# Expert rows gated in the activation and added to the stream in DRAM by accumulating indirect stores

## The chip, the cores and the metric

The kernel runs on one core of a Trainium2 chip. The metric is the device time of one execution in microseconds, 1139.73 before (median of three).

The engines are named as in the profile: PE (TensorE; PEld is its weight load), DVE (VectorE), ACT (ScalarE), POOL (GpSimd) and SP (SyncE). Each runs its own instructions in order and waits for the others by semaphores. SP, ACT and POOL can issue DMAs; an indirect DMA, whose rows go to or come from addresses in a table, is issued by POOL here.

## What is computed

One layer of a decoder for 1024 prompt rows and 64 sample rows of width 1024: a token mixing, a cross-attention, a mixture of experts and a final norm. Only the last two are touched.

```python
def hierarchical_moe(h, ...):          # h = rmsnorm(x, g_ffn)
    g_idx, g_p = top-1 of softmax over 4 expert groups
    top_v, top_i = lax.top_k(logits of the group's 4 experts, 2)
    top_w = jax.nn.softmax(top_v, axis=-1) * g_p
    gates = (one_hot(expert_id, 16) * top_w[..., None]).sum(axis=1)
    hg, hu = t @ w_gate[e], t @ w_up[e]           # 1024 -> 256
    a = jax.nn.silu(hg) * hu * gates
    return (a @ w_down[e]).summed over e          # 256 -> 1024

x = x + hierarchical_moe(rmsnorm(x, g_ffn), ...)
y = rmsnorm(x, g_final)
```

## The kernel before

The rows are held as NT = 9 tiles of 128 (the last one with 64 real rows) in the SBUF tensor X, the residual stream. The program is five blocks, each closed by a barrier of all engines: mixing, attention, routing, experts, combine.

**Routing** normalises X into xs, stores it to h_rows in DRAM (SP) and computes the router's logits. Each row goes to two experts, so there are 2176 pairs. They are sorted by expert into tiles of 128 slots, each expert beginning a tile of its own; at least MIN_TILES = 17 and at most NTILE = 32 tiles can be in use (27 are, with these inputs), and the slots left over are padding. The result is a set of small tables: IDX (the row of h_rows that each slot takes, by a matmul of the one-hot matrices big and A, line 1475), POS (the slot in which each row's two results lie), WT (the two gates of each row) and TAB (per tile: whether it starts an expert, its weights' row, whether it is in use, when the buffer is free, and the number of stores).

**Experts** works in steps, one for each tile. For tile j, POOL gathers 128 rows of h_rows into one of the two buffers of xg (`fetch`, line 1696, which waits until the tile two before is transposed), PE transposes them (`turn`, line 1822), ACT and DVE split them into a high and a low part (lines 1725 and 1785), PE multiplies by the gate and up weights (`gate_up`), ACT and DVE form a = silu(hg)*hu (lines 1740 and 1802), PE transposes a (`turn_a`, line 1845), and multiplies by the down weights (`down`). ACT copies the result into one of two buffers of y (lines 1756 and 1758) and issues its store to y_rows (line 1763). On PE step s is turn(s+1), gate_up(s), down(s-1), turn_a(s). Where a tile starts an expert, 3 MB of weights are loaded by SP in three pieces (line 1688) and split by ACT (line 1719) and DVE (line 1780) into Wh and Wl, pieces by pieces between the other work of ACT and DVE. The steps are written out for the first four tiles, then stand in loops of two steps for the rest up to 29, and again written out; from step 16 on each is skipped if its tile is empty. Each loop body begins with reads from TAB and a branch.

**Combine** has for each of the nine tiles of X: two gathers from y_rows by POS (POOL, line 1929), two multiply-adds into X with the gates WT (DVE, line 1959), a square sum (ACT, line 1950), two small operations for the norm (POOL), one for the output o (DVE, line 1969) and a store (SP).

So that combine reads defined values of y_rows, mixing ends with two copies from an input into the part of y_rows that may be left unwritten (SP, line 208).

Of the kernel before, what the change touches and what calls it, by code (L numbers as in the profile page):

```python
# [86 lines left out]
def mixing_block(nc, io, keep, y_dram):  # L87
# [10 lines left out]
    with ExitStack() as ctx:  # L98
# [32 lines left out]
        fill_st = sem("fill_st")  # L131
# [33 lines left out]
        def _(sp):  # L165
# [44 lines left out]
            sp.wait_ge(fill_st, 16 * -(-(NTILE - MIN_TILES) // NT))  # L210
# [1120 lines left out]
def routing_block(nc, io, keep, h_dram):  # L1331

    with ExitStack() as ctx:
# [3 lines left out]
        POS, WT, IDX, TAB = (keep[n] for n in ("pos", "wt", "idx", "tab"))  # L1337
# [25 lines left out]
        A = sb("A", [P, K2, NTILE])  # L1363
# [4 lines left out]
        ones_ok, h_st = sem("ones_ok"), sem("h_st", XB)  # L1368
# [68 lines left out]
        def _(pe):  # L1437
# [36 lines left out]
            for i in range(K2):  # L1474
                last = pe.matmul(ps[:, 5, 0:NTILE], big[:, i, :], A[:, i, :], start=(i == 0), stop=(i == K2 - 1))
# [3 lines left out]
        def _(dve):  # L1479
# [52 lines left out]
            then(v(WT[:, 0, :], m["gp"][:, :], m["rden"][:, :], ALU.mult))  # L1532
            then(v(WT[:, 1, :], WT[:, 0, :], m["ex"][:, :], ALU.mult))
# [33 lines left out]
            for k in range(2):  # L1567
# [12 lines left out]
            then(dve.tensor_copy(POS[:, :], pf[:, :]))  # L1580
# [3 lines left out]
            then(v(A[:, :, :], bcast(tt[:, :], NTILE), itile.rearrange("p (o n) -> p o n", o=1).to_broadcast(  # L1584
                [P, K2, NTILE]), ALU.is_equal))
            for k in range(2):
                last = v(A[:, k * NT:(k + 1) * NT, :], A[:, k * NT:(k + 1) * NT, :], bcast(tok[:, 0, :], NTILE), ALU.mult)
# [21 lines left out]
            then(r(used[:, 0:2], tef[:, :].rearrange("p (t o) -> p o t", o=2), AX_X, ALU.add))  # L1609
            then(dve.tensor_scalar(TAB[:, 4, 0:2], used[:, 0:2], 16.0, None, ALU.mult))  # L1610
            dve.wait_ge(idx_ps, 1)
            dve.tensor_copy(IDX[:, :], ps[:, 5, 0:NTILE])
# [12 lines left out]
def experts_block(nc, io, keep, h_dram, y_dram):  # L1625
# [10 lines left out]
    with ExitStack() as ctx:  # L1636
        sem = Sems(nc, keep["all"], "e")
        sb = lambda n, s, d=F32: ctx.enter_context(nc.sbuf_tensor("e_" + n, s, d))
        ps, ident, IDX, TAB = (keep[n] for n in ("ps", "ident", "idx", "tab"))
# [7 lines left out]
        x_ld, y_st = sem("x_ld", 2), sem("y_st", 2)  # L1647
# [17 lines left out]
        def tile_steps(eng, emit):  # L1665
# [5 lines left out]
            for s in range(4):  # L1671
                emit(s, s)
            for lo, hi, each in ((4, MIN_TILES - 1, emit), (MIN_TILES - 1, NTILE - 2, unless_empty)):
                with eng.Fori(0, (hi - lo) // 2) as i:
                    for u in range(2):
                        each(2 * i + (lo + u), 4 + u)
            for s in range(NTILE - 2, NTILE + 1):
                unless_empty(s, s)
# [12 lines left out]
        def _(pool):  # L1691
# [6 lines left out]
            for j in range(NTILE):  # L1698
                if j < MIN_TILES + 2:
                    fetch(j)  # L1700
                else:
                    with pool.If(started(pool, j - 2) >= 1):
                        fetch(j)

        @block.scalar
        def _(act):
# [26 lines left out]
            def step(s, like):  # L1733
# [27 lines left out]
                if like >= 1:  # L1761
                    act.wait_ge(y_ok, 2 * (s - 1) + 2)
# [3 lines left out]
            for par in range(2):  # L1766
                act.wait_ge(y_st[par], stores[par])
# [318 lines left out]
```

## Time and profile before

| | us |
|---|---|
| median of three runs (1139.54 to 1144.16) | 1139.73 |
| the profiled execution | 1139.48 |
| its span, first to last instruction | 1137.7 |
| mixing and attention | 680 |
| routing | 69 |
| experts | 333 |
| combine | 56 |

The stages are read off the timeline, at the first instruction of each block. Over the span PE is busy 83%, DVE 43%, ACT 36% and POOL 12%, and PE's granted clock is 0.924 of full speed in the mean.

The rows further down come from several views: busy time in a stretch of time; a timeline of single instructions with the idle time before each and what ended it; and groups of instructions. "issue" as a releaser means that the engine waited for nothing the profile shows. DMA times run from issue to landing.

### The profile page before, as it was taken

What the parts mean: (1) busy time and instruction counts of PE and PEld (TensorE: products, weight loads), DVE (VectorE), ACT (ScalarE), POOL (GpSimd) and SP (SyncE); (2) the same over time, 40 slices, a digit from 0 to 9 for tenths busy, and PEclk for the clock granted to TensorE, in tenths of its full rate; (3) what the DMA queues carried; (4) which work ended last, traced back from release to release, by engine and by line L of the source; (5) the groups of instructions that cost most, each with busy time, mean ns of one, the idle gap of its engine ahead of it and who ended that gap; (6) DMA issues with size and microseconds to landing.
All of it is one profiled execution on the core that took longest, in us unless ns stands there. A gap on an engine that the chain in (4) does not pass through costs nothing. (4 is left out here: it accounts for less than half of the span.)

```text
span 1137.7 us, 14742 instructions
## 1 busy us (share of the span) xinstructions
PE 938.6 (83%) x4691; PEld 763.3 (67%) x4692; DVE 484.3 (43%) x646; ACT 406.1 (36%) x657; POOL 134.7 (12%) x181
## 2 busy tenths in 40 slices
PE   4899959999989878989999989269999988769600
PEld 3689848688847665878888867158787866548500
DVE  3441373412124464733322224655554545455156
ACT  5442202300036665522111115035565545444212
POOL 3210000000011100000000004021121211001064
PEclk9999979999999989999999999659999988989955
DMA  6311010591047856100000004256868676656177
GB/s 229 146 45 64 36 44 19 236 390 40 1 170 247 309 218 259 57 28 1 1 1 1 1 1 167 78 216 221 288 249 297 232 267 219 261 204 221 56 252 256
DMA packets 40565, 171.25 MB, mean 151 GB/s; under 512 B 4971, under 2 KB 5371, under 8 KB 31658
## 3 DMA queue, kind: packets, MB, share of 16 engines
q1 hardware_dynamic: 26754, 112.74, 27.2%
q0 software_dynamic: 9872, 43.68, 11.0%
q10 hardware_dynamic: 3888, 14.16, 3.1%
q8 instruction: 32, 0.52, 0.2%
q14 instruction: 19, 0.16, 0.1%
HBM read 144.57 MB, written 33.96 MB: 157 GB/s over the span
## 5 line engine op out<-in xcount | busy, mean ns | idle before, releaser
L1780 DVE TENSOR_TENSOR e_Wl<-raw,e_Wh 128x2048 f32 x48 | 109.9, 2292 | 116.6 <-ACT e_Wh L1719 116.6
L1719 ACT CAST e_Wh<-raw 128x2048 f32 x48 | 91.7, 1912 | 95.2 <-issue 51.3
L534 PE MATMUL ps<-a_wh,a_hTh 128*128 128x512 f32 x288 | 115.8, 402 | 3.8 <-DVE a_wl L372 2.4
L535 PE MATMUL ps<-a_wh,a_hTl 128*128 128x512 f32 x288 | 113.7, 395 | 0.0
L536 PE MATMUL ps<-a_wl,a_hTh 128*128 128x512 f32 x288 | 113.5, 394 | 0.0
L1619 PE MATMUL ps<-e_Wh,e_xTh 128*128 x224 | 93.5, 418 | 0.0
L1620 PE MATMUL ps<-e_Wl,e_xTh 128*128 x224 | 90.1, 402 | 0.0
L1621 PE MATMUL ps<-e_Wh,e_xTl 128*128 x224 | 89.6, 400 | 0.0
L1696 POOL DMA_INDIRECT e_xg<-h_rows,idx x29 | 48.6, 1677 | 295.7 <-PE ps L1822 247.3
L534 PEld LDWEIGHTS ps<-a_wh,a_hTh 128*128 128x128 f32 x288 | 55.2, 192 | 15.5 <-DVE a_wl L372 2.8
L536 PEld LDWEIGHTS ps<-a_wl,a_hTh 128*128 128x128 f32 x288 | 55.0, 191 | 11.8
L535 PEld LDWEIGHTS ps<-a_wh,a_hTl 128*128 128x128 f32 x288 | 55.2, 192 | 11.1
L1822 PE MATMUL ps<-ident,e_xg 128*128 128x128 f32 x232 | 36.8, 310 | 22.2 <-issue 13.9
L1100 PE MATMUL ps<-t_QKh,t_hTh 128*128 128x512 f32 x128 | 50.6, 396 | 3.0 <-DVE t_hTl L988 2.4
L1100 PE MATMUL ps<-t_VOh,t_pTh 128*128 128x512 f32 x128 | 50.5, 395 | 2.4 <-DVE t_pTl L988 2.4
L1621 PEld LDWEIGHTS ps<-e_Wh,e_xTl 128*128 128x128 f32 x224 | 43.9, 196 | 9.9
L1619 PEld LDWEIGHTS ps<-e_Wh,e_xTh 128*128 128x128 f32 x224 | 44.3, 198 | 8.4
L1102 PE MATMUL ps<-t_QKl,t_hTh 128*128 128x512 f32 x128 | 49.9, 390 | 0.0
L1102 PE MATMUL ps<-t_VOl,t_pTh 128*128 128x512 f32 x128 | 49.9, 390 | 0.0
L1620 PEld LDWEIGHTS ps<-e_Wl,e_xTh 128*128 128x128 f32 x224 | 44.2, 197 | 8.5
L1101 PE MATMUL ps<-t_QKh,t_hTl 128*128 128x512 f32 x128 | 49.8, 389 | 0.0
L1101 PE MATMUL ps<-t_VOh,t_pTl 128*128 128x512 f32 x128 | 49.8, 389 | 0.0
(315 smaller groups left out, 1876.8 us busy)
## 6 DMA issues: line engine op xcount, KB each, us to landing
raw<-in_w_e SPq DMA_DIRECT2D x48, 1024.0 KB, 5.4
t_raw<-in_w_att SPq DMA_DIRECT2D x64, 256.0 KB, 4.1
y_rows<-e_y ACTq DMA_DIRECT2D x27, 512.0 KB, 4.4
a_raw<-in_w_mix SPq DMA_DIRECT2D x20, 512.0 KB, 6.6
t_ring<-in_kc POOLq DMA_DIRECT2D x8, 1024.0 KB, 6.3
t_ring<-in_vc POOLq DMA_DIRECT2D x8, 1024.0 KB, 8.3
a_xin<-in_x SPq DMA_DIRECT2D x9, 512.0 KB, 5.0
x<-in_x SPq DMA_DIRECT2D x9, 512.0 KB, 6.0
```

Source lines behind the costliest of these rows:

```text
L534: pe.matmul(out, hTh[:, c, own], h, start=(c == 0), stop=False)
L535: pe.matmul(out, hTl[:, c, own], h, start=False, stop=False)
L536: last = pe.matmul(out, hTh[:, c, own], l, start=False, stop=(c == KC - 1))
L1100: pe.matmul(out, xh, yh, start=start and n == 0, stop=False)
L1101: pe.matmul(out, xl, yh, start=False, stop=False)
L1102: last = pe.matmul(out, xh, yl, start=False, stop=stop and n == len(pairs) - 1)
L1619: pe.matmul(out, xh, wh, start=(n == 0), stop=False)
L1620: pe.matmul(out, xh, wl, start=False, stop=False)
L1621: last = pe.matmul(out, xl, wh, start=False, stop=(n == len(pairs) - 1))
L1696: pool.indirect_dma_start(xg[:, j % 2, :], None, h_dram[:, :], bass.IndirectOffsetOnAxis(ap=IDX[:, j:j + 1], axis=0)).then_inc(x_ld[j % 2] ...
L1719: act.copy(Wh[:, ds(off + q * PIECE, PIECE)], raw[:, q, :]).then_inc(hi_ok[q], 1)
L1780: dve.tensor_tensor(Wl[:, at], raw[:, q, :], Wh[:, at].bitcast(F32), ALU.subtract).then_inc(lo_ok[q], 1)
```

## The change

1. Routing multiplies a second copy of the one-hot table A by the gates WT (now 0 for rows that are padding of X). The matmul gives 64 columns in place of 32: row indices, and the gate of each slot (GATE). The indices are counted from 1, so that 0 marks a padding slot. From them come IDX and DST, where DST is the slot's row of the stream, or for a padding slot a row of its own in a tenth tile that nobody reads. POS is gone.
2. Routing stores X to x2_rows in DRAM (a tenth tile first, for the padding), on SP, each store ahead of that of h.
3. In the expert stage a = silu(hg)*hu*GATE (one operation of DVE with the gate as its scalar). ACT no longer stores y. POOL scatters y with addition into x2_rows by DST, each scatter waiting for the one before it to land. A copy into y waits for the scatter two before.
4. POOL's order is fetch(s+2), scatter(s-1) for each step s.
5. All steps of the expert stage are written out on PE, DVE, ACT and POOL; from step 17 on each is skipped if its tile is empty.
6. Combine loads nine plain tiles of x2_rows, half on SP and half on ACT (then g_final, on ACT), and has a buffer for each; no gathers and no multiply-adds. X is not used there.
7. Mixing has no copies into y_rows.

```diff
@@ mixing, SP
-            for lo in range(MIN_TILES, NTILE, NT):
-                n = min(NT, NTILE - lo) * P
-                sp.dma_start(y_dram[lo * P:lo * P + n, :], io["x"][0:n, :]).then_inc(fill_st, 16)
@@ routing, SP
+            sp.dma_start(x2_dram[NT * P:(NT + 1) * P, :], X[:, TS, :]).then_inc(x2_st, 16)
             for n in range(NT):
+                sp.dma_start(x2_dram[n * P:(n + 1) * P, :], X[:, n, :]).then_inc(x2_st, 16)
                 sp.wait_ge(xs_ok, n + 1)
                 sp.dma_start(h_dram[n * P:(n + 1) * P, :], xs[:, n % XB, :]).then_inc(h_st[n % XB], 16)
...
+            sp.wait_ge(x2_st, 16 * (NT + 1))
@@ routing, PE and DVE
-                last = pe.matmul(ps[:, 5, 0:NTILE], big[:, i, :], A[:, i, :], start=(i == 0), stop=(i == K2 - 1))
+                last = pe.matmul(ps[:, 5, 0:2 * NTILE], big[:, i, :], A[:, i, :, :], start=(i == 0), stop=(i == K2 - 1))
...
+            then(v(WT[:, 0, :], WT[:, 0, :], tok[:, 1, :], ALU.mult))
-            then(dve.tensor_copy(POS[:, :], pf[:, :]))
+            then(v(A[:, :, 1, :], A[:, :, 0, :], bcast(WT[:, :, :].rearrange("p k t -> p (k t)"), NTILE), ALU.mult))
...
             dve.wait_ge(idx_ps, 1)
-            dve.tensor_copy(IDX[:, :], ps[:, 5, 0:NTILE])
+            dve.tensor_copy(GATE[:, :], ps[:, 5, NTILE:2 * NTILE])
+            dve.tensor_scalar(IDX[:, :], ps[:, 5, 0:NTILE], -1.0, 0.0, ALU.add, ALU.max)
+            dve.tensor_scalar(own[:, :], tok[:, 0, 0:1], float(NT * P), None, ALU.add)
+            then(dve.tensor_scalar(spare[:, :], ps[:, 5, 0:NTILE], 0.0, None, ALU.is_equal))
+            then(dve.scalar_tensor_tensor(out=spare[:, :], in0=spare[:, :], scalar=own[:, :], in1=ps[:, 5, 0:NTILE], op0=ALU.mult,
+                                          op1=ALU.add))
+            dve.tensor_scalar(DST[:, :], spare[:, :], -1.0, None, ALU.add)
@@ experts, POOL
+            def scatter(s):
+                pool.wait_ge(y_ok, 2 * s + 2)
+                if s:
+                    pool.wait_ge(y_st, 16 * s)
+                pool.indirect_dma_start(x2_dram[:, :], bass.IndirectOffsetOnAxis(ap=DST[:, s:s + 1], axis=0), y[:, s % 2, :], None,
+                                        compute_op=ALU.add).then_inc(y_st, 16)
+
+            fetch(0)
+            fetch(1)
+            for s in range(NTILE + 1):
+                if s < MIN_TILES:
+                    if s + 2 < NTILE:
+                        fetch(s + 2)
+                    if s:
+                        scatter(s - 1)
+                else:
+                    with pool.If(started(pool, s - 1) >= 1):
...
@@ experts, ACT
-                        act.wait_ge(y_st[par], 8 * (s - 1 - par))
+                        act.wait_ge(y_st, 16 * (s - 2))
...
-                if like >= 1:
-                    act.wait_ge(y_ok, 2 * (s - 1) + 2)
-                    act.dma_start(y_dram[ds((s - 1) * P, P), :], y[:, par, :]).then_inc(y_st[par], 16)
@@ experts, DVE
-                    dve.tensor_tensor(a[:, :], sg[:, :], ps[:, 2 + like % 2, FE:2 * FE], ALU.mult).then_inc(a_ok, 1)
+                    dve.scalar_tensor_tensor(out=a[:, :], in0=sg[:, :], scalar=GATE[:, s:s + 1], in1=ps[:, 2 + like % 2, FE:2 * FE],
+                                             op0=ALU.mult, op1=ALU.mult).then_inc(a_ok, 1)
@@ combine, SP and ACT
+            for t in range(0, NT, 2):
+                sp.dma_start(x[:, t, :], x2_dram[t * P:(t + 1) * P, :]).then_inc(x_ld[t], 16)
...
+            for t in range(1, NT, 2):
+                act.dma_start(x[:, t, :], x2_dram[t * P:(t + 1) * P, :]).then_inc(x_ld[t], 16)
+            act.dma_start(gf[:, :], io["g_final"].to_broadcast([P, D])).then_inc(g_ld, 16)
```

How the order moves, at the two places that matter here. First POOL at the head of the expert stage; e_xg is the buffer of the gathered rows, e_tr_ps counts tiles transposed by PE. Before:

```order
L1696 DMA e_xg<-h_rows,idx 128x1024 x2
L1696 DMA e_xg<-h_rows,idx 128x1024 [waits e_tr_ps] x17
L1660 TENSOR_LOAD tab
L1660 ISA x2
L1702 COMPARE_AND_BRANCH
L1696 DMA e_xg<-h_rows,idx 128x1024 [waits e_tr_ps]
L1702 UNCONDITIONAL_BRANCH
```

After (x_rows is the DRAM tensor x2_rows, e_y_ok counts copies into y, e_y_st counts landed scatters):

```order
L1699 DMA e_xg<-h_rows,idx 128x1024 x2
L1699 DMA e_xg<-h_rows,idx 128x1024 [waits e_tr_ps] x2
L1705 DMA x_rows<-e_y,dst 1280x1024 [waits e_y_ok]
L1699 DMA e_xg<-h_rows,idx 128x1024 [waits e_tr_ps]
L1705 DMA x_rows<-e_y,dst 1280x1024 [waits e_y_st,e_y_ok]
L1699 DMA e_xg<-h_rows,idx 128x1024 [waits e_tr_ps]
L1705 DMA x_rows<-e_y,dst 1280x1024 [waits e_y_st,e_y_ok]
```

Gathers followed one another with PE's transposes alone between them; now each gather from the fifth on stands behind a scatter, which has waits of its own.

Second DVE in combine; c_yg are the gathered results, c_x0_ok says that the first of the two was added. Before:

```order
L1959 SCALAR_TENSOR_TENSOR x<-c_yg,wt,x 128x1024 [waits c_y_ld0]
L1959 SCALAR_TENSOR_TENSOR x<-c_yg,wt,x 128x1024 [waits c_x0_ok,c_y_ld0]
L1959 SCALAR_TENSOR_TENSOR x<-c_yg,wt,x 128x1024 [waits c_y_ld1,c_g_ld]
L1959 SCALAR_TENSOR_TENSOR x<-c_yg,wt,x 128x1024 [waits c_x0_ok,c_y_ld1]
L1969 SCALAR_TENSOR_TENSOR c_o<-x,c_st,c_gf 128x1024 [waits c_r_ok]
L1959 SCALAR_TENSOR_TENSOR x<-c_yg,wt,x 128x1024 [waits c_y_ld2]
L1959 SCALAR_TENSOR_TENSOR x<-c_yg,wt,x 128x1024 [waits c_x0_ok,c_y_ld2]
L1969 SCALAR_TENSOR_TENSOR c_o<-x,c_st,c_gf 128x1024 [waits c_r_ok]
```

After, first ACT's loads and square sums (c_x_ld0 to c_x_ld8 count landed tiles):

```order
L1938 DMA c_x<-x_rows 128x1024 x4
L1939 DMA c_gf<-in_g_final 128x1024
L1944 ACTIVATE c_junk,c_st<-c_x 128x1024 [waits c_x_ld0]
L1944 ACTIVATE c_junk,c_st<-c_x 128x1024 [waits c_sq_ok,c_x_ld1]
L1944 ACTIVATE c_junk,c_st<-c_x 128x1024 [waits c_sq_ok,c_x_ld2]
```

Then DVE, from the end of the expert stage on (the first three rows are its last branches and the barrier):

```order
L1675 COMPARE_AND_BRANCH
L1675 UNCONDITIONAL_BRANCH
L1946 UNCONDITIONAL_BRANCH [waits barrier_Pool_Activation_PE_DVE_SP_release]
L1951 SCALAR_TENSOR_TENSOR c_o<-c_x,c_st,c_gf 128x1024 [waits c_r_ok,c_g_ld]
L1951 SCALAR_TENSOR_TENSOR c_o<-c_x,c_st,c_gf 128x1024 [waits c_r_ok] x8
L1901 UNCONDITIONAL_BRANCH
```

Of three operations for each tile of X one is left, and its first stands behind the load of g_final, which is the last of those on ACT.

## Rows read from the trace of the kernel before

**Rows 1.** Engines by stage: us; busy PE, PEld, DVE, ACT, POOL; clock; DMA share; GB/s.

```profile
749.00:1082.00 333.00, 279.55 (x1284) 228.00 (x1284) 163.94 (x133) 166.87 (x189) 48.64 (x29) 0.93 0.64 230
1082.00:1137.70 55.70, 0.00 (x0) 0.00 (x0) 33.90 (x27) 10.36 (x18) 31.27 (x36) 0.50 0.75 259
```

**Rows 2.** Timeline of POOL, expert stage: start, us, line, work, [idle before <-releaser].

```profile
788.70 2.45 POOL L1696 DMA_INDIRECT e_xg<-h_rows,idx  x1 [8.49 <-PE ps L1822]
798.28 0.95 POOL L1696 DMA_INDIRECT e_xg<-h_rows,idx  x1 [7.12 <-PE ps L1822]
818.11 0.95 POOL L1696 DMA_INDIRECT e_xg<-h_rows,idx  x1 [7.66 <-PE ps L1822]
896.35 0.95 POOL L1696 DMA_INDIRECT e_xg<-h_rows,idx  x1 [7.34 <-PE ps L1822]
```

**Rows 3.** Timeline at 815 us, all engines.

```profile
815.32 0.38 PE L1845 MATMUL ps<-ident,e_a 128*128 128x128 f32 x2
816.75 1.09 PE L1822 MATMUL ps<-ident,e_xg 128*128 128x128 f32 x8 [1.05 <-issue]
817.16 0.59 ACT L1758 COPY e_y<-ps 128x512 f32<-128x512 f32 x1
```

**Rows 4.** Timeline at 787 us, all engines.

```profile
787.01 0.38 PE L1845 MATMUL ps<-ident,e_a 128*128 128x128 f32 x2
788.85 1.92 ACT L1719 CAST e_Wh<-raw 128x2048 f32 x1 [0.77 <-issue]
791.05 2.29 DVE L1780 TENSOR_TENSOR e_Wl<-raw,e_Wh 128x2048 f32 x1 [0.39 <-ACT e_Wh L1719]
791.14 0.59 ACT L1758 COPY e_y<-ps 128x512 f32<-128x512 f32 x1
```

**Rows 5.** The tile e_xg, gathers at 800 to 846 us, then 846 to 915 us.

```profile
DMA to landing us min/median/max: 5.4/7.5/9.4
...
DMA to landing us min/median/max: 5.8/9.8/10.5
```

**Rows 6.** PE alone by microsecond: busy us (instructions), clock, DMA share, GB/s.

```profile
926.00:927.00 1.00, 0.00 (x0) 0.89 0.00 0
932.00:933.00 1.00, 1.00 (x4) 0.50 1.00 410
935.00:936.00 1.00, 1.00 (x6) 1.00 0.94 389
```

**Rows 7.** Timeline of ACT at 923 us.

```profile
923.48 1.01 ACT L1725 CAST e_xTh<-ps 128x1024 fp32r<-128x1024 f32 x1
934.72 1.91 ACT L1719 CAST e_Wh<-raw 128x2048 f32 x1 [9.95 <-DMA raw<-in_w_e]
```

**Rows 8.** Timeline of ACT at the end of the expert stage.

```profile
1074.35 0.59 ACT L1758 COPY e_y<-ps 128x512 f32<-128x512 f32 x1
1075.11 0.34 ACTq L1763 DMA_DIRECT2D y_rows<-e_y  x1
1081.15 0.19 ACT L1768 COPY e_sg<-ident 1x1 f32<-1x1 f32 x1 [6.21 <-issue]
```

**Rows 9.** Timeline of the last stage.

```profile
1089.59 2.68 DVE L1959 SCALAR_TENSOR_TENSOR x<-c_yg,wt,x 128x1024 f32<-128x1024 f32 x2 [15.75 <-DMA c_yg<-y_rows,pos]
1134.30 0.56 SPq L1919 DMA_DIRECT2D out_y_s<-c_o  x1
```

**Rows 10.** The page, DMA issues: KB each, median us from issue to landing.

```profile
x<-in_x SPq DMA_DIRECT2D x9, 512.0 KB, 6.0
```

**Rows 11.** Groups by line: count, busy us, mean ns, idle before.

```profile
L1969 DVE SCALAR_TENSOR_TENSOR c_o<-x,c_st,c_gf 128x1024 f32<-128x1024 f32 x9 | 11.5, 1277 | 1.7 <-POOL c_st L1941 1.7
```

**Rows 12.** Engines in a stretch while the copies of line 208 run.

```profile
230.00:235.00 5.00, 5.00 (x24) 4.14 (x23) 0.69 (x1) 0.00 (x0) 0.00 (x0) 1.00 1.00 409
```

**Rows 13.** Timeline of DVE at the end of the routing stage.

```profile
738.29 0.75 DVE L1584 TENSOR_TENSOR r_A<-r_tt,r_cst 128x576 f32<-128x576 f32 x1
747.96 0.19 DVE L1612 CAST idx<-ps 128x32 int32<-128x32 f32 x1 [0.70 <-PE ps L1475]
```

More of the change, by code:

```diff
@@ L1336, in routing_block @@
         X, ps, ident, nhalf = keep["x"], keep["ps"], keep["ident"], keep["nhalf"]
-        POS, WT, IDX, TAB = (keep[n] for n in ("pos", "wt", "idx", "tab"))
+        IDX, DST, GATE, TAB = (keep[n] for n in ("idx", "dst", "gate", "tab"))
         K2 = 2 * NT
@@ L1362, in routing_block @@
         cmp8 = sb("cmp8", [P, K2, NTHR - 1])
-        A = sb("A", [P, K2, NTILE])
+        A = sb("A", [P, K2, 2, NTILE])
+        WT, spare, own = sb("WT", [P, 2, NT]), sb("spare", [P, NTILE]), sb("own", [P, 1])
         te, te2, base2 = sb("te", [P, NTILE, NE]), sb("te2", [P, NTILE, NE]), sb("base2", [P, NE])
@@ L1638, in experts_block @@
         sb = lambda n, s, d=F32: ctx.enter_context(nc.sbuf_tensor("e_" + n, s, d))
-        ps, ident, IDX, TAB = (keep[n] for n in ("ps", "ident", "idx", "tab"))
+        ps, ident, IDX, DST, GATE, TAB = (keep[n] for n in ("ps", "ident", "idx", "dst", "gate", "tab"))
         Wh, Wl = sb("Wh", [P, 2 * ESZ], F32R), sb("Wl", [P, 2 * ESZ], F32R)
@@ L1670, in unless_empty @@
                     emit(s, like)
[L1671 to L1678, printed above, removed]
+            for s in range(NTILE + 1):
+                if s < MIN_TILES:
+                    emit(s, s)
+                else:
+                    unless_empty(s, s)
         @block.sync
@@ L1697, in fetch @@
                                         bass.IndirectOffsetOnAxis(ap=IDX[:, j:j + 1], axis=0)).then_inc(x_ld[j % 2], 16)
-            for j in range(NTILE):
-                if j < MIN_TILES + 2:
-                    fetch(j)
-                else:
-                    with pool.If(started(pool, j - 2) >= 1):
-                        fetch(j)
+            def scatter(s):
[6 more added lines that the diff above has]
+            fetch(1)
+            for s in range(NTILE + 1):
+                if s < MIN_TILES:
+                    if s + 2 < NTILE:
+                        fetch(s + 2)
+                    if s:
+                        scatter(s - 1)
+                else:
+                    with pool.If(started(pool, s - 1) >= 1):
+                        if s + 2 < NTILE:
+                            fetch(s + 2)
+                        scatter(s - 1)
+            pool.wait_ge(y_st, pool.value_load(TAB[0:1, 4, 0:1], min_val=16, max_val=16 * NTILE))
         @block.scalar
@@ L1872, in step, with combine_block @@
                     turn_a(s, like)
[L1874 to L1895 removed]
+            last = None
+            for s in range(NTILE + 1):
+                if s < MIN_TILES:
+                    this = started(pe, s)
+                    step(s, s, last, this)
+                    last = this
+                else:
+                    last = started(pe, s - 1)
+                    with pe.If(last >= 1):
+                        step(s, s, last, started(pe, s) if s < NTILE else None)
+def combine_block(nc, io, keep, x2_dram):
     with ExitStack() as ctx:
@@ L1982, in build @@
         keep["gcol"] = sb(ctx, "gcol", [P, 4 * KC + NG])
-        keep["pos"] = sb(ctx, "pos", [P, 2 * NT], I32)
-        keep["wt"] = sb(ctx, "wt", [P, 2, NT])
+        keep["gate"] = sb(ctx, "gate", [P, NTILE])
+        keep["dst"] = sb(ctx, "dst", [P, NTILE], I32)
         keep["idx"] = sb(ctx, "idx", [P, NTILE], I32)
```

102 lines of the change are left out of this document (25 added, 77 removed).

## The prediction

> **What bounds the kernel now.** I read the busy time by stage first, then the timeline of the expert stage engine by engine, then the last stage. In the expert stage, 749 to 1082 us, PE is busy for 279.6 of 333 us and the DMA engines for 0.64 of it. In the last stage PE does nothing and the DMA engines are busy for 0.75 [rows 1]. So there are two questions: what sets the step of a tile in the first, and what sets the chain of gather, add, scale and store in the second.
>
> Step s of the expert stage is, on PE, turn(s+1), gate_up(s), down(s-1), turn_a(s). The POOL timeline gives the period: each gather is released by a turn, and from the one at 798.28 to the one at 896.35 there are ten steps, 9.81 us each or 19.6 us a pair [rows 2]. At the edge of a loop body PE stands for 1.05 us before turn with "issue" as its reason [rows 3]; without it the pair is 18.6, so PE's own step is 9.3 us. POOL waits 7 to 8 us of each step for PE and does nothing else: the gather for tile s+3 goes out right behind turn(s+1), and is wanted at turn(s+3), 18.6 us later. It lands after 7.5 us in the median of one stretch and 9.8 in the next [rows 5]. It has some 9 us to spare.
>
> **The gather loses that slack.** After the change the POOL queue alternates gather and scatter, and the gather for tile s+3 stands behind the scatter of tile s-1. That scatter waits for y(s-1), which ACT copies out only after step s has ended on PE. How late depends on the step. Where a new expert's second piece is cast between the transpose of a and y (every second step, since experts have two tiles here), turn_a ends at 787.39 and the second copy of y at 791.73, that is 4.35 us later [rows 4]. Where it isn't, it is 815.70 to 817.75, 2.05 us [rows 3]. So for the step with the cast the time from turn(s+1) to turn(s+3), both on PE, becomes a chain:
>
> 9.3 (PE's step) + 4.35 (until y is written) + 0.4 (two hand-overs; y to its store takes 0.17 [rows 8], so this is an estimate) + 2.45 (POOL issues the scatter) + 7.5 (the gather lands) = 24.0 us.
>
> For the landing I take the lower of the two medians, since the slow ones are mostly those whose issue DVE had stretched. For the scatter I take the 2.45 us of the gather at 788.70 and not the 0.95 of its neighbours [rows 2], because DVE runs its 2.29 us subtraction from 791.05 on [rows 4], just when this scatter is issued. Two things come on top. The scatter moves 512 KB ahead of the gather; at the 409 GB/s of a stretch full of copies [rows 12] this is 1.3 us as a plain transfer and 2.6 if the destination is read as well. I take 1.3. And PE now stands for about 5 us before the turn. In the trace of before its granted clock had begun to fall (0.89, from 1.00) within the microsecond 926 to 927 of an idle stretch, was at 0.50 (1.2 GHz) at 932, and back at 1.00 (2.4 GHz) at 935 [rows 6]. About four busy microseconds at half speed lose 2. Together 27.3 us a pair against 19.6, or **+7.7 us**. From 778 to 915 us there are seven such pairs: **+54 us**. In the other parity the same sum without the cast and with 0.95 for the scatter is 20.2 us, hardly more than today, and it runs inside the first.
>
> The bounds of this term: with 0.95 for the scatter, 5.4 for the landing (the least of rows 5), no queueing and no fall of the clock it is 20.4 us a pair, +0.8 or +6 us in all. With 10.5 for the landing, 2.6 for the queue and 3 for the clock it is 32.6, +13 or +91 us.
>
> The Trainium skill bears on the queueing. "DMA: Bandwidth & Descriptors", section "SWDGE vs HWDGE vs iDMA", says that accumulating transfers can be issued only from GpSimd, and its section "Queues, rings and completion order" that each DMA engine consumes one ring's descriptors in order and takes turns between rings. By it the gather cannot start before the scatter's descriptors are consumed; without it the sum would be 9 us less (1.3 a pair). No row of before has an accumulating transfer, so the trace can't confirm it.
>
> **The rest of the expert stage.** From 915 us on most experts have one tile and the weights decide: ACT casts x at 923.48 and then stands until 934.72 for the next weights, 9.95 us [rows 7]. A turn that is a few us late is hidden there; only the cover of steps in which PE runs through is gone, about three of the last twelve. Between 0 and 19 us (two and a half pairs at 7.7); I take one, **+8 us**. What hides the rest is that wait for the weights; the accumulating traffic could lengthen it, which the upper bound takes in. Taking the loops apart removes the 1.05 us of [rows 3] from a pair, but where the gather binds this is inside the chain and gives nothing. The removed store of y on ACT (0.34 us of its queue, [rows 8]) and the gate as a scalar operand on DVE I cost at nothing: down(s-1), twelve matmuls that PE runs between gate_up and turn_a, covers the latter.
>
> **Routing.** The table A gets a second half: one more multiplication the size of line 1584's (0.75 us), with small ones of 0.2 around it, in front of PE's sums, which have 64 columns in place of 32 (0 to 1 us). Behind them one conversion of 0.19 us becomes six [rows 13], with every engine waiting at the end of the block. **+2.5 us** (1.5 to 4). The ten stores of X are on SP between the stores of h; a store's buffer is wanted again three tiles later, so I take 0, with up to 1.5 us of that upper bound for them.
>
> **Between the stages.** y of the last tile is written at 1074.94. Before, its store is issued at 1075.11 and ACT goes through empty steps until 1081.15 [rows 8]. After, the scatter takes 0.95 to issue and must land, 6 to 10 us by the gathers of [rows 5], with the barrier behind it. **+2.5 us** (1 to 5).
>
> **The last stage.** Before, DVE waits 15.75 us for the first pair of gathers, the stage lasts 55.7 us at 259 GB/s, and the last store is issued at 1134.30 and leaves 3.4 us to the end [rows 1, 9]. After, there are nine plain loads and g_final, 5.24 MB, where 9.4 MB were gathered; at 409 GB/s 12.8 us, with some 1.5 for issue. g_final is last on ACT's queue, so DVE begins about 14 us in (a plain load of X landed after 6.0, [rows 10], so the squares run before that). Then nine operations of 1.28 us [rows 11], 11.5, and 3.4 for the last store: 29 us in place of 55.7, **-26.5 us**. At the 259 GB/s of the old stage the loads take 20 us and the gain is 19; if the loads spread better it is 28.
>
> **Mixing.** The fill of y_rows goes. While it runs, PE is busy for 5.00 of 5 us [rows 12] and nobody waits for it: 0.
>
> **The sum.** The profiled execution took 1139.48 us, 1.8 more than its span, and is within 0.3 us of the median. 1139.5 + 54 + 8 + 2.5 + 2.5 - 26.5 = **1180 us**. All lower bounds together: 1139.5 + 6 + 0 + 1.5 + 1 - 28 = 1120. All upper: 1139.5 + 91 + 19 + 4 + 5 - 19 = 1239.5.
>
> **Rivals.** (a) The gathers land just in time and the last stage's gain stands. For it: POOL's issue is 0.95 us in most rows and some gathers land in 5.4. Against it: those were not behind a scatter, and the weights load just then. It gives 1120 to 1134; it decides once y-to-landing stays under 10 us. This is the case of the other side, faster. (b) The scatters are the chain: each waits for the one before to land. If one takes longer than about 13 us, it sets the step. At 15 us the 15 regular steps cost 5.2 each, 78, and the last four 20 more; with the other terms of the sum it is 1139.5 + 98 + 2.5 + 2.5 - 26.5 = 1216. Nothing in the trace shows what an accumulating row costs; plain gathers at 6 to 10 speak against it. (c) The loops are what counts: each of some 13 pairs gives back 1.05 us, and the gathers stay hidden. That is 1120 less 10, 1110 us; [rows 2] speak against it, since the new order takes 9 us of the slack whatever the loops do. The Trainium skill's "Runtime: NRT & Kernel Launch", section "Instruction fetch mechanics", argues for this rival: a taken branch breaks the sequential fetch, so straight code is preferred; the 1.05 us at the loop's edge agrees with it in direction. (d) As the forecast, but nearly balanced by the last stage, 1134 to 1146.
>
> **Chances.** Forecast 0.64 (its own range 1148 to 1220), (a) 0.14, (b) 0.11, (c) 0.05, (d) 0.06. A measurement of this kernel can tell about 0.5%, 5.7 us. Faster by more than that: (a) and (c), 0.20. Within it: most of (d) 0.06. Slower: 0.74. The range of 1122 to 1230 us leaves out (c) and the far ends.
>
> **What would show it.** Right: in the profile after, PE idle before turn on the landing of e_xg, in every second step, 4 to 6 us; gathers issued right behind a scatter; seven pairs of about 27 us; a last stage near 29 us whose DVE begins with g_final. Wrong: turns without a wait for DMA (then (a) or (c)), or POOL waiting for its own scatter to land (then (b)). The weakest number is the landing of gather and scatter, next to it the clock.

## The result, and the profile after

The changed kernel took 1181.96 us (median of 4 runs, 1172.87 to 1182.43), the kernel before 1141.95 us beside it: a ratio of 1.0325, with a 95% interval from 1.0291 to 1.036. It is slower. The profiled execution took 1181.91 us, with a span of 1180.0 us.

The stages after, as windows (from, to, length, busy time of PE, PEld, DVE, ACT and POOL with the number of instructions, granted clock, share of the DMA engines, GB/s):

```profile
680.00:752.00 72.00, 42.77 (x291) 34.56 (x289) 40.16 (x118) 20.82 (x38) 12.57 (x19) 0.76 0.46 183
752.00:1150.00 398.00, 292.30 (x1284) 240.01 (x1284) 165.88 (x133) 167.10 (x189) 102.11 (x57) 0.86 0.66 195
1150.00:1180.00 30.00, 0.00 (x0) 0.00 (x0) 10.87 (x9) 10.34 (x18) 7.68 (x18) 0.50 0.84 324
```

Against [rows 1] the last stage is some 26 us shorter and the expert stage 65 us longer. What PE waits for there, and what POOL waits for (the waits of the whole span: total, times, longest):

```profile
PE ps L1835 <- DMA e_xg<-h_rows,idx: 83.0, 16, 7.5
POOL x_rows L1705 <- ACT e_y L1776: 237.4, 21, 19.0
POOL x_rows L1705 <- DMA x_rows<-e_y,dst: 36.3, 6, 6.6
```

Before, PE waited once for a gather in this stage. Now it does so 16 times, 83 us in all. This is one pair of steps of the long stretch, from the timeline of the engines (start, duration, instruction, and in brackets the idle time ahead of it with what ended it):

```profile
871.11 1.04 PE L1835 MATMUL ps<-ident,e_xg 128*128 128x128 f32 x8
875.02 0.59 ACT L1776 COPY e_y<-ps 128x512 f32<-128x512 f32 x1
875.89 2.80 POOL L1705 DMA_INDIRECT x_rows<-e_y,dst  x1 [12.60 <-ACT e_y L1776]
879.00 0.98 POOL L1699 DMA_INDIRECT e_xg<-h_rows,idx  x1 [0.30 <-issue]
886.50 2.29 POOL L1705 DMA_INDIRECT x_rows<-e_y,dst  x1 [6.52 <-DMA x_rows<-e_y,dst]
886.98 1.97 PE L1835 MATMUL ps<-ident,e_xg 128*128 128x128 f32 x8 [6.40 <-DMA e_xg<-h_rows,idx]
889.10 0.98 POOL L1699 DMA_INDIRECT e_xg<-h_rows,idx  x1 [0.30 <-PE ps L1835]
898.31 1.04 PE L1835 MATMUL ps<-ident,e_xg 128*128 128x128 f32 x8
```

Read it as a chain: y is written at 875.61, the scatter goes out at 875.89 and takes 2.80 us to issue, the gather behind it goes out at 879.00 and lands 8.0 us later, and only then does PE turn the next rows, after 6.40 us of nothing. The step after this one finds its rows in place. The second scatter waits 6.52 us for the first to land, but nobody waits for the gather behind it. Each scatter of this parity comes 27.2 us after the last (821.57, 848.81, 875.89, 903.09, 930.29, 957.54). PE's idle time also costs its clock, which was 1.00 up to 884 us (two windows of one microsecond, in the wait and after it):

```profile
886.00:887.00 1.00, 0.02 (x1) 0.03 (x1) 1.00 (x1) 0.00 (x0) 0.50 (x1) 0.50 0.14 57
891.00:892.00 1.00, 1.00 (x6) 0.82 (x5) 0.25 (x1) 0.00 (x0) 0.00 (x0) 0.93 1.00 303
```

At 886 the granted clock is 0.50 (1.2 GHz), and it is back near 1.00 (2.4 GHz) at 891. The end of the timeline after, which answers to [rows 8, 9]:

```profile
1142.03 1.59 POOL L1705 DMA_INDIRECT x_rows<-e_y,dst  x1 [7.49 <-ACT e_y L1776]
1149.79 2.21 ACTq L1938 DMA_DIRECT2D c_x<-x_rows  x4
1152.03 0.51 ACTq L1939 DMA_DIRECT2D c_gf<-in_g_final  x1
1164.94 10.87 DVE L1951 SCALAR_TENSOR_TENSOR c_o<-c_x,c_st,c_gf 128x1024 f32<-128x1024 f32 x9 [24.32 <-DMA c_gf<-in_g_final]
1175.84 0.57 SPq L1922 DMA_DIRECT2D out_y_s<-c_o  x1
```

To say where the time lies I cut the expert stage by the moment at which ACT has written y of a tile: tile 0, tile 13 (the end of the stretch with two tiles to an expert) and tile 26 (the last). These are the rows of the second copies of y of tiles 0 and 13 before (that of tile 26 is in [rows 8]), then of tiles 0, 13 and 26 after:

```profile
779.61 0.59 ACT L1758 COPY e_y<-ps 128x512 f32<-128x512 f32 x1
908.50 0.58 ACT L1758 COPY e_y<-ps 128x512 f32<-128x512 f32 x1
```

```profile
782.33 0.59 ACT L1776 COPY e_y<-ps 128x512 f32<-128x512 f32 x1
956.68 0.58 ACT L1776 COPY e_y<-ps 128x512 f32<-128x512 f32 x1
1141.03 0.59 ACT L1776 COPY e_y<-ps 128x512 f32<-128x512 f32 x1
```

The same cut of all kernels that the argument uses, in us, each from its own profiled execution:

| kernel | tile 0 to 13 | tile 13 to 26 | span |
|---|---|---|---|
| before | 128.9 | 165.9 | 1137.7 |
| after | 174.3 | 184.4 | 1180.0 |
| e4: before, loops written out | 123.4 | 166.8 | 1137.8 |
| e2: after, scatter of 64 columns | 160.0 | 170.1 | 1150.4 |
| e3: after, no addition | 170.0 | 170.9 | 1159.4 |
| e1: after, gather first | 129.3 | 173.0 | 1122.5 |
| e8: gather first, no addition | 126.4 | 159.3 | 1102.8 |
| e9: gather first, two streams | 124.3 | 173.0 | 1122.1 |

Every row is one execution, so small differences mean little. e6 and e10, further down, share the expert stage of e1 and have 127.5 and 130.0, then 172.1 and 170.3: up to 2.7 us apart with the same instructions. e5, with the scatters of e9, has 124.1 and 167.1.

### The profile page after: what moved, and what is told of

It reads as the page before. It is cut to its first block and busy times, and to the rows that moved or that the text cites. A ratio compares the mean times of both kernels' runs of the same rounds, so it can differ in the third digit from the quotient of the medians.

```text
span 1180.0 us, 14260 instructions
## 1 busy us (share of the span) xinstructions
PE 953.1 (81%) x4691; PEld 776.8 (66%) x4691; DVE 464.5 (39%) x633; ACT 406.1 (34%) x656; POOL 164.4 (14%) x191
## 3 DMA queue, kind: packets, MB, share of 16 engines
q0 software_dynamic: 11312, 48.92, 14.5%
## 5 line engine op out<-in xcount | busy, mean ns | idle before, releaser
L1835 PE MATMUL ps<-ident,e_xg 128*128 128x128 f32 x232 | 43.7, 351 | 85.8 <-DMA e_xg<-h_rows,idx 83.0
L1705 POOL DMA_INDIRECT x_rows<-e_y,dst x27 | 64.3, 2382 | 273.7 <-ACT e_y L1776 237.4
L1625 PE MATMUL ps<-e_Wh,e_xTh 128*128 x224 | 98.2, 438 | 0.0
L1835 PEld LDWEIGHTS ps<-ident,e_xg 128*128 128x128 f32 x232 | 35.5, 181 | 90.6 <-DMA e_xg<-h_rows,idx 87.2
L1626 PE MATMUL ps<-e_Wl,e_xTh 128*128 x224 | 93.5, 418 | 0.0
L1627 PE MATMUL ps<-e_Wh,e_xTl 128*128 x224 | 92.7, 414 | 0.0
L1625 PEld LDWEIGHTS ps<-e_Wh,e_xTh 128*128 128x128 f32 x224 | 47.4, 212 | 9.3
L1626 PEld LDWEIGHTS ps<-e_Wl,e_xTh 128*128 128x128 f32 x224 | 46.7, 209 | 9.2
```

Source lines behind the costliest of these rows:

```text
L1625: pe.matmul(out, xh, wh, start=(n == 0), stop=False)
L1626: pe.matmul(out, xh, wl, start=False, stop=False)
L1627: last = pe.matmul(out, xl, wh, start=False, stop=(n == len(pairs) - 1))
L1705: pool.indirect_dma_start(x2_dram[:, :], bass.IndirectOffsetOnAxis(ap=DST[:, s:s + 1], axis=0), y[:, s % 2, :], None, compute_op=ALU.add). ...
L1835: last = pe.transpose(ps[:, c // 4, c % 4 * P:(c % 4 + 1) * P], xg[:, like % 2, c * P:(c + 1) * P], ident[:, :])
```

## The experiments

The theory was that the order on POOL's queue costs the time: the gather for tile s+3 stands behind the scatter of tile s-1, which waits for y. The rivals were the traffic of the scatters, their waiting for one another, and the loops.

**e1, the gather ahead of the scatter.** Only the order on POOL's queue changes; nothing else waits on a gather for tile s+3 than the turn two steps on.

```diff
             fetch(0)
             fetch(1)
+            fetch(2)
...
-                    if s + 2 < NTILE:
-                        fetch(s + 2)
+                    if s + 3 < NTILE:
+                        fetch(s + 3)
                     if s:
                         scatter(s - 1)
```

> The changed kernel with one thing moved: on POOL the gather for tile s+3 is issued before the scatter of tile s-1, behind turn(s+1), where it stood before the change. Everything else is as after. The theory (the gather's place in the queue costs the expert stage its 65 us): no wait of turn for the gather is left in the regular stretch, a pair of steps takes 18.6 to 19.6 us in place of 27.2, the expert stage 325 to 345 us in place of 398, the kernel 1112 to 1130 us. Rival, the scatters are the chain (one lands 10 us after its issue and each waits for the one before): two of them a pair still set it, 1150 us or more. Rival, accumulating traffic slows weights and gathers whatever the order: 1135 to 1150 us.

Measured: 1125.44 us (median of 4), a ratio to before of 0.9873 (0.9817 to 0.9928). That is 56 us less than after, and faster than before. PE's waits for gathers fall from 83.0 us to 9.7 (waits of e1, 752 us on), and POOL now waits for its own scatters:

```profile
PE ps L1836 <- DMA e_xg<-h_rows,idx: 9.7, 4, 6.4
POOL x_rows L1705 <- DMA x_rows<-e_y,dst: 80.9, 12, 8.0
```

The order is the cause of most of what the expert stage lost. The table says how much where: 45.0 us from tile 0 to 13 (174.3 to 129.3), and 11.4 from tile 13 to 26.

**e2, a scatter of 64 columns.** Each scatter keeps its order, its addition and its 128 rows but moves 64 of the 1024 columns, to a small tensor of its own. The expert rows are left out of the output.

```diff
-                pool.indirect_dma_start(x2_dram[:, :], ..., y[:, s % 2, :], None,
+                pool.indirect_dma_start(few[:, :], ..., y[:, s % 2, 0:64], None,
```

> The changed kernel with the scatter moving 64 of the 1024 columns, into a small tensor of its own that routing also fills (ten small stores more). It leaves the experts' results out of the output. POOL still issues 128 rows with addition, waits for y and for the landing of the scatter before. It takes away the transfer in front of the gather and keeps the order and the issue. The theory prices that transfer at 1.3 us a pair (2.6 if the destination is read as well): gathers land 6.5 to 7 us after issue in place of 8.0, a pair takes 25 to 26.3 us, the kernel 1165 to 1175 us. Rival, the traffic of the scatters is the cause and not the order: 1120 to 1140 us.

Measured: 1152.19 us (one run), span 1150.4. That lies between the two: the bytes together with their addition cost about 30 us, well over my theory's, and with them gone the span is still 12.7 us over that of before. POOL's groups and DMA issues of e2 (the last number of the second and third row is the median from issue to landing):

```profile
L1707 POOL DMA_INDIRECT few_rows<-e_y,dst x27 | 59.8, 2213 | 243.9 <-ACT e_y L1778 224.5
few_rows<-e_y,dst POOLq DMA_INDIRECT x27, 4.4
e_xg<-h_rows,idx POOLq DMA_INDIRECT x30, 5.6
```

The issue of the scatter costs 2.2 us though it moves a sixteenth, and in the pairs' chain it is 2.80 as in after; the bytes don't set that. The gather behind it lands after 5.6 us in place of 8.0. Six pairs of 2.4 us are 14.4, and from tile 0 to 13 e2 is 14.3 us shorter than after. So being queued with a full scatter costs a gather 2.4 us; I had put 1.3. The other 14.3 us lie between tiles 13 and 26, where I had expected nothing. e2 takes away bytes and addition at once; e3 parts them.

**e3, a scatter that writes and doesn't add.** Same bytes, same rows, same order; the addition is left out, so that of a token's rows the last one stands.

```diff
-                                        compute_op=ALU.add).then_inc(y_st, 16)
+                                        ).then_inc(y_st, 16)
```

> The changed kernel with the scatters overwriting rows in place of adding to them (the output is then not the sum). It measures what the addition costs a transfer of 128 rows of 4 KB. The theory takes 1.3 us of the other half of the destination's reading at most: a scatter lands 8 to 9.5 us after issue in place of 10, a pair 26 to 27 us, the kernel 1172 to 1181 us. Rival, addition is slow on the DMA engines: 1150 us or less.

Measured: 1161.28 us (one run), span 1159.4, some 20 us less than after and outside what I expected. The addition shows on the page in the DMA queues (packets, MB, and the time of the packets as a share of 16 engines' span). After, then e3:

```profile
q0 software_dynamic: 11312, 48.92, 14.5%
x_rows<-e_y,dst POOLq DMA_INDIRECT x27, 9.5
```

```profile
q0 software_dynamic: 11312, 48.92, 10.9%
x_rows<-e_y,dst POOLq DMA_INDIRECT x27, 4.6
```

Packets and bytes are the same. The time is 14.5% of 1180.0, or 171.1 us of all 16 engines, against 10.9% of 1159.4, or 126.4. The additions take 44.7 us of all engines, 1.7 us for each of the 27 scatters of 512 KB. The two medians of the landing, 9.5 and 4.6 us, overstate what the addition costs one scatter, because each is taken over two different stretches. Among the pairs (issued from 800 us to tile 13) a scatter lands after 9.8 us with the addition and 8.6 without; behind tile 13 it is 7.3 and 4.5.

In the pairs my theory held: 26.4 us each, and the scatter's landing as I had put it. There the addition costs 4.3 us of the table (its scatter is issued in 2.80 us and not 2.19, and the gather behind lands in 8.0 us and not 7.5). The excess is 13.5 us between tiles 13 and 26, nearly all of the 14.3 that e2 gained there. What PE and ACT wait for in that stretch is this, in after (957 to 1142 us) and in e3 (952 to 1123 us):

```profile
PE ps L1835 <- DMA e_xg<-h_rows,idx: 39.8, 8, 7.5
ACT e_Wh L1737 <- DMA raw<-in_w_e: 39.0, 12, 12.7
```

```profile
PE ps L1834 <- DMA e_xg<-h_rows,idx: 27.5, 8, 5.3
ACT e_Wh L1736 <- DMA raw<-in_w_e: 32.6, 12, 10.6
```

Without the additions both the gathers and the weights come sooner: 12.3 us less waiting for the first and 6.4 for the second.

**e4, the kernel before with its loops written out.** Nothing else is taken from the change.

```diff
-            for s in range(4):
-                emit(s, s)
...
+            for s in range(NTILE + 1):
+                if s < MIN_TILES:
+                    emit(s, s)
+                else:
+                    unless_empty(s, s)
```

> The kernel before with only its expert stage written out in steps as the change does it, no loops; gathers, stores and the last stage as before. By the gap of 1.05 us at the edge of a loop body, 13 pairs give back at most 13 us, less where the weights decide: 1127 to 1133 us. If the loops had no part in the time: 1138 to 1142 us. If straight code is fetched more slowly: above 1142 us.

Measured: 1139.2 us (median of 10), a ratio of 0.9968 (0.9942 to 0.9994). That lies in the range that I had given for loops with no part in the time, and the interval leaves out 1 only just. The gap at a loop's edge is worth less than I gave it: from tile 0 to 13 the stage is 5.5 us shorter, 0.9 a pair, and from tile 13 to 26 it is 0.9 longer, which is within the spread. That the weights set the pace there is my reading and not tested. This profiled execution reached its first gather at 754.99 us, 5.9 later than before; its steps ahead of the routing stand in the same code, so I take that for the spread between executions and use only lengths inside the stage.

**e5 and e9, two streams of scatters.** In e1 each scatter still waits for the one before to land, because two tiles may hold rows of one token. Here odd tiles go to a second tensor, and a scatter waits only for the one two before. The rows of the odd tiles are left out of the output. This is the edit of both, on the kernel of e1:

```diff
-                if s:
-                    pool.wait_ge(y_st, 16 * s)
-                pool.indirect_dma_start(x2_dram[:, :], ...
+                if s >= 2:
+                    pool.wait_ge(y_st[s % 2], 16 * (s // 2))
+                pool.indirect_dma_start((x2_dram, odd)[s % 2][:, :], ...
```

> The kernel of e1 (gather of row s+3 issued ahead of the scatter of row s-1), with the scatters of odd tiles sent to a second DRAM tensor, so that no scatter waits for the one before it, only for the one two before, whose buffer it is. The rows of the odd tiles are left out of the output; the second tensor is filled with 4.6 MB more in the mixing stage. In e1 the scatters of the long stretch stood 9.90 us apart (804.08 to 912.94, 11 steps), each behind the landing of the one before (80.9 us in 12 waits), where the steps of before stood 9.3 apart. Theory (the wait for the previous landing is what e1 still loses, 11 x 0.3 to 0.6): 1119 to 1122, and the steps at 9.3. Rival (the DMA engines, busy 0.83 of that stretch, are what stretches it, and two scatters side by side move the same bytes): 1124 to 1129, steps still near 9.8, landings longer than 8.6.

Measured: 1136.87 us (median of 10), ratio 0.9962 (0.9937 to 0.9986), slower than either theory had it. The experiment had two faults of mine. The fill of the second tensor stood in the routing block and not in mixing, ahead of the stores on SP's queue, and the stage began 13.7 us late. And the end of the stage waited in branches for the last landings. The timeline of e5 shows the second (ACT's last operation, then the first load of the last stage):

```profile
1091.88 0.19 ACT L1788 COPY e_sg<-ident 1x1 f32<-1x1 f32 x1 [4.54 <-issue]
1105.13 2.75 SPq L1924 DMA_DIRECT2D c_x<-x_rows  x5
```

From one start to the other it is 13.3 us; in e1 it is 3.7. In between, the steps did come 9.4 us apart. In e9 the fill goes out behind the routing's stores, and the end waits on two values:

```diff
+            n16 = pool.value_load(TAB[0:1, 4, 0:1], min_val=16, max_val=16 * NTILE)
+            pool.wait_ge(y_st[0], (n16 + 16) // 32 * 16)
+            pool.wait_ge(y_st[1], n16 // 32 * 16)
```

> e5 again without its two faults. There the 4.6 MB that fill the second tensor stood ahead of the routing's stores on SyncE's queue (first gather at 765.02 instead of 751.37), and the branches that wait for the last landings at the end of the stage kept the last stage back (ScalarE done at 1091.88, first load at 1105.13, 13.3 us; in e1 3.7). Now the fill is issued after the routing's stores, and the end waits on two register values. Rows of odd tiles are again left out of the output. Theory (the wait for the previous landing is what e1 loses in the long stretch): from the first gather to the last scatter 323 us as in e5 against 332.8 in e1, so 10 us less than e1 in all: 1114 to 1118. Rival (the order of the fill moved other things in e5, and the gain was an artefact): 1123 to 1128.

Measured: 1120.06 us (median of 4), ratio 0.9793 (0.9765 to 0.982), against 0.9873 for e1. In its profiled execution (span 1122.1) tile 0 to 13 takes 124.3 us in place of 129.3; tile 13 to 26 takes 173.0 in both. So the wait for the previous landing costs e1 some 5 us (3 to 6 against e6, e1 and e10), in the stretch where PE sets the step and there only. The profiled spans of e1 and e9 are nearly equal all the same, since the fill makes e9's first gather 3.9 us later. The whole gain is some 6 to 9 us by the ratios (against e10, e6 and e1), less than the 10 I had taken from e5: a part of those stood behind the regular stretch, and e9 didn't repeat it.

**e7, two streams in the changed kernel's own order.** The same edit, with e5's fill and end, on the changed kernel.

> The changed kernel with its own order on GpSimd's queue (scatter first, then the gather), and the scatters of odd tiles sent to a second tensor as in e5 (rows of odd tiles left out of the output). This takes the wait for the previous landing (36.3 us in 6 waits of GpSimd) away and leaves the gather behind the scatter. Theory (the pair chain runs through ScalarE's copy of y, one scatter's issue and one gather's landing; the wait for the previous landing stands beside it, and frees only a gather that nobody waits for): 1176 to 1184, pair period still 27. Rival (scatters one after the other are the chain): the pair shrinks by the 6.5 of that wait, 7 x 6.5 = 45 less: 1135 to 1145.

Measured: 1200.36 us (one run), span 1198.6, above both. The fill costs 8.3 us here (first gather at 760.91 against 752.57) and the branches at the end 9.7 (from the last y to the first load 17.9 against 8.2), which is the excess. The expert stage itself doesn't move: from the first gather to the last scatter 390.2 us, after 389.5. The pairs keep their period (scatters of e7; the third row begins the next pair):

```profile
885.29 2.80 POOL L1707 DMA_INDIRECT odd_rows<-e_y,dst  x1 [17.31 <-ACT e_y L1783]
892.36 1.59 POOL L1707 DMA_INDIRECT x_rows<-e_y,dst  x1 [2.98 <-ACT e_y L1783]
912.52 2.82 POOL L1707 DMA_INDIRECT odd_rows<-e_y,dst  x1 [17.29 <-ACT e_y L1783]
```

The second scatter goes out as soon as y is there, 7.1 us behind the first and not 10.6, and the pair is 27.2 us as ever. The serial scatters are not what bounds the changed kernel, and rival (b) of the prediction is out.

**e8, the gather first and no addition.** The edits of e1 and e3 together, with the additions left out of the output as in e3.

> The kernel of e1 with the scatters writing instead of adding (the additions are left out, the bytes written are the same). In e3 such a scatter landed 4.6 us after its issue against 8.6 with the addition, and DESCRIPTORS took 2.2 instead of 2.8 us beside VectorE. Theory (with the right order only the serial landing matters, and 4.6 + 2.3 fits into a step of 9.3): waits of GpSimd for the previous landing near zero, steps at 9.3, 1118 to 1122. Rival (in e3 the missing addition gave 20 us through the DMA engines that it freed, whatever the order): 1105 to 1112.

Measured: 1104.71 us (one run), span 1102.8. My theory gave 1118 to 1122, the rival 1105 to 1112; the rival is right, by its lower edge. My theory also had POOL's waits for its own scatters near zero. They are 46.9 us in 7 waits, against 80.9 in 12: I had taken the landing of 4.6 us from e3's median, and among the pairs it is 8.4 here. Against e1 the stretch of regular steps gains 2.9 us, tile 13 to 26 gains 13.7, and the end 2.7 (the last scatter lands sooner). Without the addition the changed kernel was 4.3 and 13.5 us shorter in the two stretches (e3). So the addition costs some 13.6 us between tiles 13 and 26 in either order. With the gather first, the weights are what is late there (e1's PE waits 1.1 us for a gather behind tile 13). ACT's wait for them (930 to 1100 us) and their landing (925 to 1090 us), in e1 and in e8:

```profile
ACT e_Wh L1738 <- DMA raw<-in_w_e: 58.0, 14, 12.7
raw<-in_w_e SPq DMA_DIRECT2D x19, 1024.0 KB, 8.3
```

```profile
ACT e_Wh L1737 <- DMA raw<-in_w_e: 39.5, 11, 11.0
raw<-in_w_e SPq DMA_DIRECT2D x18, 1024.0 KB, 6.7
```

A load of 1 MB lands 1.6 us later when additions run beside it, and ACT waits 18.5 us longer for weights. In the kernel before, that load took 5.3 us in the same window.

**e6 and e10, g_final first.** In after and in e1 DVE starts only when g_final has landed, behind all other loads. e6 is e1 with that load issued first on ACT's queue; e10 also lets DVE begin only at the fifth row.

```diff
+            act.dma_start(gf[:, :], io["g_final"].to_broadcast([P, D])).then_inc(g_ld, 16)
             for t in range(1, NT, 2):
                 act.dma_start(x[:, t, :], ...
-            act.dma_start(gf[:, :], io["g_final"].to_broadcast([P, D])).then_inc(g_ld, 16)
```

> The kernel of e1 with one line moved in the last stage: g_final's load is issued ahead of the loads of x rows on ACT's queue, not behind them. In e1 VectorE's first output pass starts at 1107.50, released by that load, when eight of the nine tiles' sums have long been ready (the first c_x landed by 1097.2). Theory: passes then follow the sums, one each 1.24 us from about 1099.5, and the last (its x row lands by 1107.3) sets the end: 1109.5 + 1.2 instead of 1118.4, so 6 to 8 us less than e1: 1117.5 to 1120. Rival: stores from 1101 on share the DMA engines with the loads still on their way, the last x rows land later by as much, and only 2 to 4 us are saved: 1121.5 to 1124.

Measured: 1127.5 us (median of 6), ratio 0.9863 (0.9831 to 0.9896), no different from e1 and above both ranges. DVE begins at once, but each of its passes now waits for POOL (two of e6's rows):

```profile
1113.85 1.28 DVE L1952 SCALAR_TENSOR_TENSOR c_o<-c_x,c_st,c_gf 128x1024 f32<-128x1024 f32 x1 [0.72 <-POOL c_st L1933]
1115.85 1.28 DVE L1952 SCALAR_TENSOR_TENSOR c_o<-c_x,c_st,c_gf 128x1024 f32<-128x1024 f32 x1 [0.72 <-POOL c_st L1933]
```

A pass every 2.00 us in place of 1.20 uses up what the early start gave. From the first load to the end it is 29.6 us, in e1 30.3.

```diff
             dve.wait_ge(g_ld, 16)
+            dve.wait_ge(r_ok, 2 * 5)
```

> The kernel of e6 (g_final first on ScalarE's queue), and VectorE begins its output passes only when five of the nine rows' factors are there. In e6 VectorE began at 1102.35, with the first factor, and from then on GpSimd's two small operations and VectorE's pass took turns: a pass every 2.00 us (idle 0.72 before each, released by GpSimd), the last at 1119.85. In e1 VectorE began with eight factors there and ran at 1.20. Theory (the two engines hold each other up while both run): five factors by about 6.5 us after the first, then five passes of 1.2 while the last four factors come at about 2.0: last pass at 15 to 16 us after the first row has landed instead of 19.9, so 3 to 5 us less than e1: 1120 to 1123. Rival (GpSimd's small operations are slow there for another reason, such as the stores, and come at 2.0 from the first store on): within 1 us of e1, 1124 to 1127.

Measured: 1124.18 us (median of 6), ratio 0.9847 (0.9822 to 0.9872), span 1119.5. From the first load to the end it is 29.4 us, 0.9 less than e1, where I had expected 3 to 5. Eight of the nine passes run at 1.2 us without a gap, and the last waits 0.44 us for POOL, whose two small operations take 0.76 and 1.47 us beside the passes and 0.19 and 0.55 alone. But the passes begin 9.5 us after the first row has landed and not 6.5: with g_final ahead of them the second row landed 3.5 us behind the first. e1, e6 and e10 can't be told apart by time. All three are faster than both kernels and leave nothing of the output out.

## Why the prediction was right, and where it wasn't

The forecast of 1180 us met 1181.96. Its sum can be checked term by term, since the two spans differ by 42.3 us:

| term | predicted | measured | from |
|---|---|---|---|
| pairs of regular steps | +54 | +45.4 | tile 0 to 13 |
| rest of the expert stage | +8 | +18.5 | tile 13 to 26 |
| routing | +2.5 | +3.4, and -0.7 up to tile 0 | first gather 752.57 against 749.13 |
| between the stages | +2.5 | +1.3 | y written to first load, 8.2 against 6.9 |
| last stage | -26.5 | -25.6 | first load to the end, 30.2 against 55.8 |

- **The chain of the pair** was right in its steps and nearly in each size. One lap, from the turn at 859.89 to the one at 886.98, is 11.4 us to the end of turn_a (predicted 9.3 with 2 for the clock), 4.34 until y is written (4.35), 0.6 for the hand-overs (0.4), 2.80 for the scatter's issue (2.45) and 8.0 for the gather's landing (7.5, with 1.3 for the queue): 27.1 us. The shares were off inside the landing: the scatter's company costs 2.4 us of it by e2 (1.9 of them without the addition, by e3) where I had 1.3, and behind the small scatter the gather lands in 5.6 and not 7.5. Why [rows 5] have 7.5, with weights loading beside the gathers in both, no run settles; the two errors cancelled. That e1 took the term back, by 45.0 of 45.4 us, shows its cause.
- **The count of the pairs** was off. There are six and not seven between tiles 1 and 13, at 7.6 us each; the seventh belongs to the stretch behind.
- **The rest of the stage** is the term that failed in its reason. I costed it by turns that come late and let the additions in only as an upper bound. The runs give two parts: the order costs 11.4 us (184.4 to 173.0, e1), and the addition 13.6 (e3, e8). e1 takes away 38.7 us of PE's waits for gathers behind tile 13 (39.8 to 1.1) and meets 23.4 us more of ACT's for the weights (39.0 to 62.4), so the weights hid only a part of the late turns. Together the parts are 25 us, and yet the stage is only 18.5 over before: with both taken out, in e8, it is 6.6 us shorter than before. What gives those 6.6 us is not settled. The written-out loops don't (e4: +0.9). The stores of y that no longer go out from ACT's queue, and the gate in the activation, were not tried alone. So this term came out 10.5 us too low, the pairs 8.6 too high, and the sum owes its closeness to that: luck, not method.
- **The addition** was the blind spot. No row of before had one, and I charged it to one place, 1.3 to 2.6 us ahead of a gather. It takes 1.7 us of all DMA engines each time, and behind tile 13 it delays the gathers and the weights (e3), and with the gather first the weights alone (e8).
- **The loops** were costed at nothing inside the chain. The chain above leaves no room for them in the changed kernel, though no run put them back there. In before they cost 0.9 us a pair (e4), near the 1.05 of [rows 3], but only over the six pairs. Rival (c) had 10 us for them and gathers that stay hidden; both failed.
- **The last stage** is 30.2 us for 29: DVE begins 15.2 us after the first load (predicted 14), its nine passes take 10.9 (11.5), and 4.2 are left to the end (3.4).
- **Rival (a)** fell, since in the pairs every second gather behind a scatter lands late. Its sum, gathers in time and the last stage's gain kept, is close to e1's time.
- **The rule on the queues**, from the Trainium skill's "DMA: Bandwidth & Descriptors", section "Queues, rings and completion order", that a ring's descriptors are taken in order, agrees with e2 in direction: with the scatter cut to a sixteenth the gather behind it lands 2.4 us sooner. The runs don't show whether that is the order in a ring or the engines' time.
- **The rule on straight code**, from the Trainium skill's "Runtime: NRT & Kernel Launch", section "Instruction fetch mechanics", agrees with e4 by 0.9 us a pair in the regular stretch, and by 0.3% of the whole. Whether it is the fetch that takes this time, no run shows.

## What to carry to other kernels

When an operation is put into a queue, look at what stands behind it and by when that is wanted; the loss here was not the new operation but the gather that it held back, and two lines that let the gather go first turned +3.2% into -1.3%. An addition on the way to DRAM is not free, though no compute engine is busy with it: price it in DMA time, and look for its cost where the transfers already set the pace. And a fix for a wait moves the bound only to the next one (POOL's landings in e1, POOL's small operations in e6), so read the next wait before counting the gain.

## What the runs showed of the hardware

- An accumulating indirect store of 128 rows of 4 KB lands 9.8 us after its issue among the pairs and 7.3 behind tile 13, a writing one 8.6 and 4.5 (after and e3), with the same packets. With the gather first it is 9.2 and 7.4 against 8.4 and 4.6 (e1 and e8). In the share of the queue this is 1.7 us of 16 engines for each (44.7 us for 27; e1 against e8 gives 174.0 and 127.9 us, also 1.7).
- POOL takes 1.59 us to issue an accumulating store where DVE is idle (1142.03), and 2.80 where DVE's 2.29 us subtraction of the weights runs (874.94 to 877.23, beside the scatter at 875.89). In e1 it took 1.59 at 864.05, beside DVE's 1.22 us operation that reads PSUM (864.00). A writing store takes 0.98, and 2.19 beside the subtraction (its longest in e3 is 2.99). The number of bytes makes no difference there: 2.80 with 64 columns too (e2).
- POOL's two small operations and DVE's pass hold each other up when each row's pass needs its factor: 2.00 us a row in e6. Where the factors were ready DVE keeps 1.2 us a pass and POOL alone is slowed (0.76 and 1.47 us in place of 0.19 and 0.55, e10).
